# HGRN core head by head with both directions in one PSUM bank; RWKV scans with four gram banks and another ScalarE order

## The reference, cut to what matters

```
# RWKV-7, 8 heads of 64, both directions, outputs added
S_t = S_{t-1} diag(w_t) + (S_{t-1} (-kk_t)) (kk_t * a_t)^T + v_t k_t^T ;  y_t = S_t r_t
y = rwkv7_scan(..., reverse=False) + rwkv7_scan(..., reverse=True)

# HGRN2, 4 heads of 128, both directions, outputs added
S_t = diag(f_t) S_{t-1} + k_t v_t^T ;  o_t = S_t^T q_t
o = o_f + flip(o_b)
```

## Time and profile before

| | before |
|---|---|
| median of 3 runs | 3788.16 us |
| profiled execution, its own time | 3786.09 us |
| its span | 3783.9 us |
| TensorE busy | 3622.2 us (96%) |
| VectorE busy | 1968.7 us (52%) |
| ScalarE busy | 1595.2 us (42%) |
| GpSimd busy | 372.8 us (10%) |
| mean granted clock of TensorE | 0.978 |

### The profile page before, as it was taken

One profiled execution on the slowest core, in us unless ns is written; L12 is line 12 of the kernel. 1 busy time (PEld: TensorE's weight loads), 2 busy tenths in 40 slices (PEclk: granted clock), 3 DMA queues, 4 the chain that ended last, 5 costly groups with the idle time before them and its releaser, 6 DMA issues. The chain is left out here.

```text
span 3783.9 us, 52344 instructions
## 1 busy us (share of the span) xinstructions
PE 3622.2 (96%) x20562; PEld 2855.0 (75%) x20562; DVE 1968.7 (52%) x3146; ACT 1595.2 (42%) x2552; POOL 372.8 (10%) x337
## 2 busy tenths in 40 slices
PE   8998889869999999999999999999999999999998
PEld 5456777658878887887777778887887777788887
DVE  5769665583443334756555453333755545453332
ACT  5754433544332333444444433323444444433322
POOL 0027323000011111010000001100010000001100
PEclk9999989979999999999999999999999999999999
DMA  3011002203332232122222232333212212233232
GB/s 120 17 53 57 2 2 70 66 13 124 92 103 95 96 96 87 62 68 69 66 84 76 84 103 95 99 93 96 67 62 68 69 54 101 84 100 100 94 95 78
DMA packets 84160, 289.33 MB, mean 76 GB/s; under 512 B 9200, under 2 KB 9456, under 8 KB 82672
## 3 DMA queue, kind: packets, MB, share of 16 engines
q1 hardware_dynamic: 83520, 283.68, 23.6%
q10 hardware_dynamic: 432, 2.78, 0.2%
HBM read 284.32 MB, written 2.10 MB: 76 GB/s over the span
## 5 line engine op out<-in xcount | busy, mean ns | idle before, releaser
L500 DVE TENSOR_TENSOR weights_lo_r<-raw_weights,weights_hi_r 128x1024 fp32r<-128x1024 f32 (+2 forms) x554 | 638.8, 1153 | 1281.8 <-ACT weights_hi_r L494 1281.6
L494 ACT ACTIVATE weights_hi_r<-raw_weights 128x1024 fp32r<-128x1024 f32 (+2 forms) x554 | 546.9, 987 | 1299.4 <-PE ps L573 1245.2
L572 PE MATMUL ps<-xn_r,weights_hi_r 128*128 128x512 f32 x2688 | 1053.8, 392 | 0.0
L571 PE MATMUL ps<-xn_hi,weights_hi_r 128*128 128x512 f32 x1632 | 667.8, 409 | 31.5 <-DVE weights_lo_r L500 9.1
L573 PE MATMUL ps<-xn_hi,weights_lo_r 128*128 128x512 f32 x1632 | 643.1, 394 | 0.0
L572 PEld LDWEIGHTS ps<-xn_r,weights_hi_r 128*128 128x128 f32 x2688 | 509.7, 190 | 106.7 <-issue 6.2
L571 PE MATMUL ps<-y_r,weights_hi_r 128*128 128x512 f32 x1200 | 470.8, 392 | 2.1 <-PEq L908 2.1
L573 PE MATMUL ps<-y_r,weights_lo_r 128*128 128x512 f32 x1200 | 467.8, 390 | 0.0
L571 PEld LDWEIGHTS ps<-xn_hi,weights_hi_r 128*128 128x128 f32 x1632 | 310.7, 190 | 125.2 <-issue 47.6
L573 PEld LDWEIGHTS ps<-xn_hi,weights_lo_r 128*128 128x128 f32 x1632 | 310.6, 190 | 68.0
L571 PEld LDWEIGHTS ps<-y_r,weights_hi_r 128*128 128x128 f32 x1200 | 225.9, 188 | 54.2 <-issue 5.2
(11 more groups left out here) (571 smaller groups left out, 5223.9 us busy)
## 6 DMA issues: line engine op xcount, KB each, us to landing
raw_weights<-in_w_ffn_dram SPq DMA_DIRECT2D x132, 512.0 KB, 3.7
raw_weights<-in_w_down_dram SPq DMA_DIRECT2D x48, 512.0 KB, 3.5
raw_weights<-in_w_out_dram SPq DMA_DIRECT2D x24, 512.0 KB, 3.6
raw_weights<-in_w_down_dram SPq DMA_DIRECT2D x24, 384.0 KB, 3.1
raw_weights<-in_w_hgrn_dram SPq DMA_DIRECT2D x16, 512.0 KB, 3.5
raw_weights<-in_w_mix_ssm_dram SPq DMA_DIRECT2D x16, 512.0 KB, 3.7
raw_weights<-in_w_a_qk_dram SPq DMA_DIRECT2D x16, 512.0 KB, 3.4
raw_weights<-in_w_mix_a_dram SPq DMA_DIRECT2D x16, 512.0 KB, 3.5
```

Of the source, the lines that this page charges most:

```text
L494: act.activation(self.k.w_hi[:, g % 2, 0:chunk.width], self.k.raw[:, slot, 0:chunk.width], ACT.Copy)\
L500: dve.tensor_tensor(self.k.w_lo[:, g % 2, 0:chunk.width], self.k.raw[:, slot, 0:chunk.width], self.k.w_hi[:, g % 2, 0:chunk.width].bitcast ...
L571: pe.matmul(out, w_hi, x_hi, start=start, stop=False)
L572: pe.matmul(out, w_hi, x_lo, start=False, stop=False)
```

## The change

HGRN core: the units go head by head (u even forwards, u odd backwards; `back`, `tile`). The backward output is accumulated onto the forward one in bank 7. ScalarE copies the sum to y (`keep_output`), TensorE turns it through bank 2, which v shares, and ScalarE copies it back. VectorE's eight output instructions are gone.

RWKV scans: four gram banks (0, 1, 2, 7). `outputs` issues the products of v with ARK ahead of the wait for Z. The exponentials of the next unit go one by one between ScalarE's Z copies. The SSM root is made in unit 0 ahead of the input copy; gram 3 waits for it. `keep_busy` is moved behind ARBS, and its number goes from 5 to 3.

```diff
-    gram_bank = lambda n: n % 3
+    GRAM_BANKS = (0, 1, 2, 7)
+    gram_bank = lambda n: GRAM_BANKS[n % len(GRAM_BANKS)]
...
             def free_gram(n):
-                if n >= 3:
-                    pe.wait_ge(gram_used, n - 2)
+                if n >= 4:
+                    pe.wait_ge(gram_used, n - 3)
+                elif n == 3:
+                    pe.wait_ge(ssm_logs, 1)
...
             def inputs(v):
                 n = TURNS * v + AVS
                 pe.wait_ge(turned_used, TURNS * v + VS + 1)
+                free_turn(n)
+                if v == 0:
+                    keep_busy(k, pe, bank(k.ps, turn_bank(n)), 3)
                 pe.wait_ge(gram_used, GRAMS * v + AKS + 2)
-                free_turn(n)
...
             def outputs(v):
-                pe.wait_ge(turned_used, TURNS * v + ZS + 2)
                 pe.wait_ge(gram_used, GRAMS * v + ARKS + 2)
...
+                free_gram(GRAMS * v + YS)
                 for j in range(NT):
                     c = slice(j * P, (j + 1) * P)
                     for h in range(2):
+                        pe.matmul(k.ps[head(h), gram_bank(GRAMS * v + YS), c], v_tok[:, j, head(h)], ARK[h][:, j, :],
+                                  start=(j == 0), stop=False, skip_group_check=True)
+                pe.wait_ge(turned_used, TURNS * v + ZS + 2)
+                for i, col, alone in ((QS, 0, True), (YS, 64, False)):
+                    n = GRAMS * v + i
+                    if alone:
+                        free_gram(n)
+                    for j in range(NT):
+                        c = slice(j * P, (j + 1) * P)
+                        for h in range(2):
+                            mm = pe.matmul(k.ps[head(h), gram_bank(n), c], Z[h][:, j, col:col + 64], ARB[h][:, j, :],
+                                           start=alone, stop=(alone or j == NT - 1), skip_group_check=True)
+                    mm.then_inc(gram_done, 1)
...
-                if v == 0:
-                    keep_busy(k, pe, bank(k.ps, gram_bank(ARBS)), 5)
...
+                yield
                 act.activation(bt, L[:, u, :], ACT.Exp, scale=HALF).then_inc(e_ready, 1)
+                yield
...
+                if v == 0:
+                    act.wait_ge(ssm_summed, 2)
+                    act.activation(ssm_rstd, bank(k.ps, 7), ACT.Ln, bias=k.const("eps")[:, 0:1], scale=1.0 / SSM_INNER)\
+                        .then_inc(ssm_logs, 1)
+                    act.wait_ge(ssm_logs, 1)
+                    act.activation(ssm_rstd, ssm_rstd, ACT.Exp, scale=-0.5).then_inc(ssm_root, 1)
+                take(v, AVS, Z4[:, :, :, 64:128], lambda ps: ps.rearrange("p (h j n) -> p h j n", h=2, j=NT),
+                     2 if back else 1)
+                if not back:
+                    tanh(Q + v)
+                steps = exps(v + 1) if v + 1 < UNITS else iter(())
+                next(steps, None)
+                take(v, ZS, Z[0], tile4)
+                next(steps, None)
+                take(v, ZS + 1, Z[1], tile4)
+                next(steps, None)
+                for c in range(NT):
+                    take_state(v, c)
+                if v + 1 < UNITS:
+                    rt_exp(v + 1)
...
+                def keep_output(h):
+                    act.wait_ge(out_done, 2 * h + 2)
+                    act.activation(y[:, h, :], bank(k.ps, 7), ACT.Copy).then_inc(y_kept, 1)
+
                 def take_output(h):
                     act.wait_ge(y_turned, h + 1)
-                    act.activation(y[:, h, :], bank(k.ps, 7), ACT.Copy).then_inc(y_ready, 1)
+                    act.activation(y[:, h, :], bank(k.ps, 2), ACT.Copy).then_inc(y_ready, 1)
...
+                    if back(u) and u > 1:
+                        keep_output(u // 2 - 1)
                     take_inputs(u)
-                    if u - 2 >= HH:
-                        take_output(u - 2 - HH)
-                take_output(HH - 2)
+                    if back(u) and u > 1:
+                        take_output(u // 2 - 1)
+                keep_output(HH - 1)
                 take_output(HH - 1)
...
-                    if u >= 2:
-                        output(u - 2)
-                        yield
...
                     pe.wait_ge(masked, u + 1)
-                    if u > HH:
-                        pe.wait_ge(y_ready, u - HH)
-                    elif u:
-                        pe.wait_ge(y_kept, u)
+                    if u > 1 and not back(u):
+                        pe.wait_ge(y_kept, u // 2)
...
                 def turn_output(h):
-                    pe.wait_ge(y_added, h + 1)
+                    pe.wait_ge(y_kept, h + 1)
+                    pe.wait_ge(v_taken, min(h + 2, HH))
...
-                        mm = pe.transpose(k.ps[:, 7, c], y[:, h, c], k.const("ident"))
+                        mm = pe.transpose(k.ps[:, 2, c], y[:, h, c], k.const("ident"))
...
-                    if u - 2 >= HH:
-                        turn_output(u - 2 - HH)
+                    if back(u) and h:
+                        turn_output(h - 1)
                     if u:
                         output(u - 1)
-                turn_output(HH - 2)
                 output(UNITS - 1)
                 turn_output(HH - 1)
```

More of the change, by code:

```diff
@@ L2897, in _ @@
                 take(v, KHS, kh_tok, tile4)
[L2898 to L2909, removed]
                 if v == 0:
@@ L3222, in _ @@
                     kh_tok, v_tok = parts(u)[6:8]
-                    if u < HH:
-                        act.wait_ge(v_turned, u + 1)
+                    if not back(u):
+                        act.wait_ge(v_turned, u // 2 + 1)
                         act.activation(v_tok, bank(k.ps, 2), ACT.Copy).then_inc(v_taken, 1)
@@ L3239, in _ @@
             def _(dve):
-                def output(w):
-                    dve.wait_ge(out_done, w + 1)
-                    h = w % HH
-                    if w >= HH:
-                        dve.tensor_tensor(y[:, h, :], y[:, h, :], bank(k.ps, 7), ALU.add).then_inc(y_added, 1)
-                    else:
-                        dve.tensor_copy(y[:, h, :], bank(k.ps, 7)).then_inc(y_kept, 1)
                 def prepare(u):
@@ L3250, in prepare @@
                     step, end, mid = marks(u)
[L3251 to L3252 removed]
+                    reset = k.const("reset")[:, back(u) * T:(back(u) + 1) * T]
+                    dve.tensor_tensor_scan(L[:, ::step], reset[:, ::step], log_f[:, tile(u), ::step], 0.0, ALU.mult,
                                            ALU.add).then_inc(prep, 1)
@@ L3268, in mask @@
                     dve.tensor_tensor(tiles(parts(w)[5]), tiles(bank(k.ps, 0)),
-                                      wide(k.const("c_ge" if w >= HH else "c_le"), NT), ALU.mult).then_inc(masked, 1)
+                                      wide(k.const("c_ge" if back(w) else "c_le"), NT), ALU.mult).then_inc(masked, 1)
                 def between(u):
@@ L3316, in _ @@
                     list(work)
-                output(UNITS - 1)
             @block.tensor
@@ L3323, in output @@
                     pe.wait_ge(masked, u + 1)
-                    if u > HH:
-                        pe.wait_ge(y_ready, u - HH)
-                    elif u:
-                        pe.wait_ge(y_kept, u)
+                    if u > 1 and not back(u):
+                        pe.wait_ge(y_kept, u // 2)
                     for j in range(NT):
                         c = slice(j * P, (j + 1) * P)
-                        pe.matmul(k.ps[:, 7, c], sc[:, c], v_tok[:, c], start=(j == 0), stop=False,
+                        pe.matmul(k.ps[:, 7, c], sc[:, c], v_tok[:, c], start=(j == 0 and not back(u)), stop=False,
                                   skip_group_check=True)
@@ L3336, in output @@
                         mm = pe.matmul(k.ps[at:at + CH, 7, j * P:(j + 1) * P], qb[:, CH * c:CH * c + CH],
-                                       S[:, order(u)[i], :], start=False, stop=(i == NC - 2), skip_group_check=True,
+                                       S[:, order(u)[i], :], start=False, stop=(i == NC - 2 and back(u) == 1), skip_group_check=True,
                                        tile_position=(0, at))
```

58 lines of the change are left out of this document (23 added, 35 removed).

## The result

The changed kernel takes **3763.06 us** (median of 4 runs, 3760.83 to 3770.01), the kernel before on the same chip 3788.8 (3786.74 to 3789.74). The ratio is 0.9931, 95% interval 0.9919 to 0.9943: 22 to 31 us faster. Forecast were 3762.4, within 3756 to 3774.

A forecast was written before the change was run, and what follows sets the result against it. TensorE's waits bound the scans, VectorE's queue HGRN. Scans 15.3, clock 1.5 and HGRN 9.0 make 25.8 us off the profiled 3786.1, 3760.3; plus 2.1 to the median gives 3762.4 us, range 3756 to 3774.

The forecast's parts named there:

- bank: Scans: with a fourth gram bank ARBS follows AKS at once and `inputs` starts 0.61 us earlier a unit, 4.9 us.
- `outputs`: Scans: eight output matmuls placed ahead of the wait for ScalarE's Z copy save 0.72 us a unit, 5.8 us.
- second transfers: Scans: the second transfer pair no longer waits for VectorE to take the first transfer bank, 0.5 a unit, 4.0 us.
- GpSimd's give-back: Scans: TensorE waits for GpSimd's factors in shorter units, about -0.1 us a unit, -0.6 us.
- rival A: Scans bound by GpSimd and ScalarE: a unit saves 0.8 in place of 1.83 us, 3769.5 us; chance 0.12.
- Clock: Forward scan units: fewer TensorE gaps bring back 1.5 us of time lost at low clock, between 0 and 3.3.
- Table load: Scans: load moves into ScalarE's idle time, ending unit 1's wait, +1.2 us; first unit's wait for Ln costed at nothing.
- First state steps: HGRN iterations: steps 10.0 and 10.4 us apart in place of 10.70, 3.0 us saved before the last iteration.
- The end: HGRN, last full iteration to last output copy: VectorE's waits for outputs go, 7.3 us saved.
- TensorE's queue at 1.2 GHz: HGRN: `turn_output` waits for ScalarE's keep and delays work behind it, -1.3 us in all (0 to -3.5).
- Rival B: HGRN: `turn_output`'s wait holds back output, next transposes and ScalarE, 4.5 us more than forecast, 3767 us; chance 0.15.
- Rivals C and D: C: less keep-busy work lowers the scans' clock, 3810 us, chance 0.04; D: waits reappear on other lines, 3788, chance 0.03.

The follow-up runs named there:

- the last test: Changed kernel with GpSimd starting at the first exponential, spreading copies on GpSimd behind both product groups, and HGRN's output kept ahead of the exponentials: 3760.16 us, ratio 0.9920.

## Why the prediction was right, and where it was not

**Bound and method: right.** In the scans TensorE's waits, in HGRN VectorE's queue. That the time is 0.7 us off the forecast is luck. At a like clock the scans' work gave 10 to 11 us and not 15.3; about 2 more than forecast from the clock, 0.5 more from HGRN and 0.9 from the rest of the program made up for most of it, and the profiled execution lay 1.5 below its median where I had taken 2.1.

**Scans, bank, `outputs`, second transfers: mechanism right, size right where nothing else binds.** By the table of units above, units 0 and 5 gain 2.00 and 1.94 for 1.83. ARBS follows AKS at once, `inputs` starts 2.62 us after AKS and not the 2.51 forecast.

**GpSimd's give-back: the step that failed.** "Slack 0.2 + 1.5 - 1.83 leaves about -0.1 a unit: -0.6", and "+1.2" for unit 1. The chain was taken at its old length of 5.88; moved forward, it met VectorE's copies and became 6.38. TensorE waited 0.85 in unit 1 (forecast: nearly none) and 0.68 and 0.32 in units 6 and 7. In a unit without a wait the transposes of b start 0.93 us after the unit's first; in the kernel before they were 1.45 late in unit 1 alone, now they are 1.00, 0.26, 0.84 and 0.49 late in units 1, 2, 6 and 7. The two terms, +0.6 together, come to -1.1 instead. This was rival A's engine at a quarter of its price (7.1), in four units. That unit 5 is free of it because the stop in unit 4 gave GpSimd time is argued, not shown.

**Not foreseen: the "issue" stops.** Before there were 0.5, 0.7 and 0.2 us of them beside the transfer waits (units 2, 4, 7); after, these three:

```profile
457.53 0.27 PE L2776 MATMUL ps<-weights_lo 32*64 32x64 f32 x2 [1.04 <-issue]
...
527.84 0.27 PE L2776 MATMUL ps<-weights_lo 32*64 32x64 f32 x1 [1.03 <-issue]
...
576.38 0.21 PE L2776 MATMUL ps<-weights_lo 32*64 32x64 f32 x1 [1.03 <-issue]
```

The waits removed had covered part of them: there the second transfer pair's 0.5 was given back. Smaller stops, of about 0.3 us, came in units 1 and 6. Of the 3 us between 11.7 and 8.8 about 1.7 are the stops and 1.4 is GpSimd. Unit 7 with its chain, which the table below the last test leaves out, went from 39.83 to 39.59 us at the same granted clock of 0.96: 0.24 for 1.73, again a longer stop and GpSimd.

The traces show what the stops go with. Counting TensorE's matmuls and weight loads, 51 of the 52 stops in these fourteen executions' scans come at places that are multiples of 256 apart (the three above at 5825, 8385 and 10435, each within three of such a place). Each of the 51 ended 2.2 to 2.8 us after a packet of 16 KB had begun on a DMA queue that the profile calls "instruction"; for the first stop it is this one, begun at 455.21, and for the others one begun at 525.58 and at 574.12, 2.3 us earlier every time:

```profile
q8 instruction: 1, 0.02, 5.5%
```

In the transfers TensorE's instructions are many and short. The stretch of 256 that ends at the first stop took 3.14 us with the scan code of before (the run with HGRN's part alone, 0.43 of it a stop) and 3.03 in the changed kernel (1.04 of it), though a wait of 0.35 had gone. So TensorE most likely waits there for its own next instructions, and to take away a wait that such a stop covers gains nothing. That is read off the times; no run changed the number of instructions to test it.

**Clock: right sign, size not separable.** I allowed 1.5 (0 to 3.3). About 3 us of the scans' 13.8 are clock, but the profiled execution of before was a poor one: two later executions of the same scan code took 205.2 and 206.2. The bound of 3.3 was drawn too tight: it came from the forward units, while over all the scans the granted clock was 0.93, 29 us at 1.2 GHz and not 6.6. My price of a half at most for a low microsecond holds (0.26 and 0.37 here).

**Table load: right.** Unit 0 has no load before its exponentials any more, and ARBS waits 0.47 for Ln where I took nothing, at most 1.3.

**HGRN: right in each term.** First state steps 738.00 to 798.48 are 60.48 us where they were 751.82 to 815.42, 63.60: 3.12, forecast 3.0. The end: 24.56 to the merge's first matmul, now 18.20: 6.36, forecast 7.3 less about 1.2 for TensorE's queue at 1.2 GHz. (The pieces that I listed for the end add up to +15.75 and not to +16.0; the last copy started at +17.30.) The final products ran at 1.2 GHz in fact (1.93 us for 1.07). Rival B did not come: TensorE's waits of 1.6 and 3.4 us for the kept output lie where it had nothing else due; with the copy moved ahead of the exponentials they are gone, and HGRN is 0.63 shorter, the two odd periods. (B's own sum, 3 x 1.0 + 2.5 less the 1.3 already taken, is 4.2 and not 4.5.)

**Rivals C and D: out.** The granted clock of the forward units rose from 0.96 to 0.98, with six keep-busy records for ten. Whether the idles that went away did it is open: one and the same scan code, with the same waits, had 0.93 in one execution and 0.98 in another.

## What to carry to other kernels

When a chain on GpSimd is moved, ask which VectorE instructions within SBUF it will now run beside, and take neither its old length nor theirs. A wait that is removed is worth its length only in those rounds of the loop in which no other engine is nearly as late, so price the edits by unit and not times eight. Where a stretch of very short TensorE instructions stops without a releaser, compare the stop with the packets of the instruction queue before you count on a wait beside it. Judge an effect of a few us by stage lengths at a like granted clock, and put the work that must move in the gap where its engine is idle and nobody waits.

## What the runs showed of the hardware

Four VectorE copies of 32x256 within SBUF took 1.59 us in the changed kernel and 4.28 us against running GpSimd products; a GpSimd copy and product 0.21 and 1.25 us alone, 0.44 and 1.49 when the VectorE copies ran first. The same four copies on GpSimd take 2.67 us. TensorE's granted clock differed between executions of the same code by 0.04 to 0.05 over the scans, worth 5.5 to 6.2 us. Stops of TensorE with no releaser in the profile come at the transfers (L2776) in units 2, 4 or 7 of every kernel: 0.2 to 0.7 us with three gram banks, 0.8 to 1.6 with four. They stand 256 of TensorE's instructions apart or a multiple of it, and end 2.2 to 2.8 us after a 16 KB packet has begun on the instruction queue; that they are a wait for instructions is inferred, not tested.
